# A two-layer hybrid trunk on one core: another order of work in the kernel's first microseconds

## The reference, cut to what matters

```python
h = rmsnorm(x, norm1_g[l])
x = x + mixing_block(h, cos, sin, w_in[l], ...)      # p = h @ w_in, four branches on column groups of p,
                                                     # y_b = branch_b @ w_branch[b], gated by sigmoid(h @ w_gate), then @ w_o
h = rmsnorm(x, norm2_g[l])
x = x + hier_moe(h, ...)                             # 16 experts, top 1 group of 4, top 2 experts inside it
```

## Time and profile before

| what | value |
|---|---|
| timed runs, median (lowest to highest) | 839.33 us (838.76 to 840.03), 3 runs |
| the profiled execution's own time | 837.2 us |
| its span, first to last instruction | 835.5 us |
| PE busy | 789.1 us, 94% |
| DVE busy / ACT busy / POOL busy | 79% / 61% / 2% |
| mean granted clock of TensorE | 0.975 of full speed |
| read from memory | 188.12 MB |

### The profile page before, as it was taken

The page is one execution under the profiler, slowest core; times in us unless marked ns, Lnnn a source line. Parts: engine busy times, 40 slices in busy tenths (PEclk is TensorE's granted clock), DMA queues, the critical chain, the costliest instruction groups (busy, mean ns, idle before and its releaser), DMA issues.

```text
span 835.5 us, 13286 instructions
## 1 busy us (share of the span) xinstructions
PE 789.1 (94%) x4822; PEld 698.7 (84%) x4822; DVE 660.5 (79%) x854; ACT 512.1 (61%) x567; POOL 20.0 (2%) x32
## 2 busy tenths in 40 slices
PE   6999999999779999999799999999958999999996
PEld 6899999998558877877789999999846878787875
DVE  5858996497567889989774899559756889988987
ACT  5535555653537778777543555664454787878774
POOL 3110000000000000000001000000000000000000
PEclk9999999999879999999999999999987999999998
DMA  7867254366215999999645644337521899999994
GB/s 245 293 202 249 84 175 150 102 243 211 101 51 204 339 347 331 356 342 325 215 144 200 206 147 153 127 102 276 167 88 48 282 322 362 334 350 348 352 342 172
DMA packets 80309, 189.80 MB, mean 227 GB/s; under 512 B 12022, under 2 KB 23944, under 8 KB 80264
## 3 DMA queue, kind: packets, MB, share of 16 engines
q1 hardware_dynamic: 80264, 189.20, 65.5%
HBM read 188.12 MB, written 1.05 MB: 226 GB/s over the span
## 4 chain that ended last, share of the span: by engine, by line
PE 63%; issue 23%; ACT 5%; DVE 5%; DMA 2%; POOL 1%; SPq 0%; ACTq 0%; DVEq 0%; POOLq 0%
PE bank L1244 18%; PE bank L1246 18%; PE bank L1245 18%; ACT w_hi L482 3%; PE bank L1539 2%; PE bank L1568 2%; DVE w_lo L743 2%; PE bank L1593 1%; DMA raw<-in_w_in 1%; DMA raw<-in_w_e_up 1%; DMA raw<-in_w_e_down 1%; PE bank L1512 1%; ACT xn L493 1%; ACT a_hi L661 0%; DVE gates L1180 0%
## 5 line engine op out<-in xcount | busy, mean ns | idle before, releaser
L743 DVE TENSOR_TENSOR w_lo<-raw,w_hi 128x2048 fp32r<-128x2048 f32 (+1 forms) x183 | 403.1, 2217 | 91.8 <-ACT w_hi L482 90.7
L482 ACT ACTIVATE w_hi<-raw 128x2048 fp32r<-128x2048 f32 (+1 forms) x183 | 338.8, 1857 | 180.5 <-PE bank L1246 136.6
L1244 PE MATMUL bank<-a_hi,w_hi 128*128 128x256 f32 x704 | 201.2, 286 | 4.0 <-DVE a_lo L818 4.0
L1245 PE MATMUL bank<-a_hi,w_lo 128*128 128x256 f32 x704 | 199.8, 284 | 0.0
L1246 PE MATMUL bank<-a_lo,w_hi 128*128 128x256 f32 x704 | 199.7, 284 | 0.0
L1244 PE MATMUL bank<-w_hi,y_lo 128*128 128x512 f32 x432 | 171.4, 397 | 0.5 <-DVE w_lo L743 0.2
L1246 PE MATMUL bank<-w_lo,y_lo 128*128 128x512 f32 x432 | 168.8, 391 | 0.0
L1244 PEld LDWEIGHTS bank<-a_hi,w_hi 128*128 128x128 f32 x704 | 135.6, 193 | 5.2 <-DVE w_lo L743 3.6
L1245 PEld LDWEIGHTS bank<-a_hi,w_lo 128*128 128x128 f32 x704 | 135.7, 193 | 0.1
L1246 PEld LDWEIGHTS bank<-a_lo,w_hi 128*128 128x128 f32 x704 | 135.6, 193 | 0.0
L1245 PE MATMUL bank<-w_hi,y_hi 128*128 128x512 f32 x288 | 112.3, 390 | 0.0
(11 more groups left out here) (288 smaller groups left out, 872.2 us busy)
## 6 DMA issues: line engine op xcount, KB each, us to landing
raw<-in_w_e_gate SPq DMA_DIRECT2D x72, 512.0 KB, 4.4
raw<-in_w_e_up SPq DMA_DIRECT2D x72, 512.0 KB, 5.8
raw<-in_w_e_down SPq DMA_DIRECT2D x72, 512.0 KB, 4.9
raw<-in_w_gate SPq DMA_DIRECT2D x56, 512.0 KB, 4.6
raw<-in_w_in SPq DMA_DIRECT2D x38, 512.0 KB, 6.5
raw<-in_w_branch SPq DMA_DIRECT2D x16, 512.0 KB, 4.1
raw<-in_w_o SPq DMA_DIRECT2D x16, 512.0 KB, 4.2
raw<-in_w_gate SPq DMA_DIRECT2D x16, 256.0 KB, 2.9
```

What stands on the lines that cost most here:

```text
L482: a.activation(w_hi[:, at.slot(n, PART), 0:w], raw[:, slot, 0:w], ACT.Copy).then_inc(hi_done, 1)
L743: v.tensor_tensor(w_lo[:, part, 0:w], raw[:, slot, 0:w], w_hi[:, part, 0:w].bitcast(F32), ALU.subtract).then_inc(split_done, 1)
L1244: mm(ps, a2[0], b2[0], start=first, stop=False, skip_group_check=shared)
L1245: mm(ps, a2[1], b2[0], start=False, stop=False, skip_group_check=shared)
```

## The change

- SP: unit 0 is requested right behind x; then come g1, units 1 and 2, unit 3 (which stood behind all parameters), `positions` (which stood ahead of g1), and then the parameters.
- ACT: an activation of one element right at the start, whose function is the one that x's squares use, so that the function table is loaded there. Unit 3's `hi` stands ahead of the sine of the angles.
- DVE: `lo` of unit 0 stands behind the fourth slice of h_lo, no longer ahead of the first. `lo` of unit 3 stands ahead of the rotary angles.
- PE: in layer 0 six more products of ones (`keep_warm(3, 6)`) follow the transposes, into bank 3. Units 0 and 1 are multiplied in another order: first all products with w_hi (hi*hi and h_lo*w_hi; 32 matmuls), which wait for `hi` alone, then those with w_lo (16 matmuls), which wait for `lo`. The products and their number are as before.

```diff
             for t in range(T):
                 sp.dma_start(x[:, t, :], x_in[0, P * t:P * t + P, :]).then_inc(x_loaded[t], 16)
-            sp.dma_start(posi[:, :], positions[0].rearrange("(t p) -> p t", p=P),
-                         allow_slow_non_contiguous=True).then_inc(pos_loaded, 16)
...
+            load(At(0, 0, False), 0, *units_a[0], 0)
             norm_gains(0)
-            first_units(At(0, 0, False), 0)
+            first_units(At(0, 0, False), 0, 1)
+            load(At(0, 0, False), AHEAD, *units_a[AHEAD], 0)
+            sp.dma_start(posi[:, :], positions[0].rearrange("(t p) -> p t", p=P),
+                         allow_slow_non_contiguous=True).then_inc(pos_loaded, 16)
             mixer_parameters(0)
             router_parameters(0)
...
+            act.wait_ge(pool_consts, 1)
+            a.activation(warm[:, 0:1], ones[0:1, 0:1], ACT.Square)
             act.wait_ge(S("ssq_zero"), 1)
...
                     hi(at, 1)
                     hi(at, 2)
+                    hi(at, AHEAD)
                     act.wait_ge(S("angles"), 1)
...
-            lo(At(0, 0, False), 0)
...
+                    if l == 0 and k == 3:
+                        lo(At(0, 0, False), 0)
...
                     lo(at, 1)
                     lo(at, 2)
+                    lo(at, 3)
                     rope_angles()
...
+                if l == 0:
+                    keep_warm(3, 6)
...
+                def first_products(at, n, h, wp):
+                    ks = [4 * h + kk for kk in range(4)]
+                    pe.wait_ge(hi_done, at.unit(n) + 1)
+                    for kk, k in enumerate(ks):
+                        pe.wait_ge(S("h_lo_done"), KT * l + k + 1)
+                        for hp in H:
+                            for f in range(2):
+                                mm(bank[0][:, 256 * f:256 * f + 256], wp[0][:, kk, P * f:P * f + P], hp[:, k, :],
+                                   start=k == 0 and f == 0 and hp is h_hi, stop=False, skip_group_check=True)
+                            for t in range(T):
+                                mm(bank[1][:, 256 * t:256 * t + 256], hp[:, k, P * t:P * t + P], wp[0][:, kk, 256:512],
+                                   start=k == 0 and t == 0 and hp is h_hi, stop=False, skip_group_check=True)
+                    ready(at, n)
+                    for kk, k in enumerate(ks):
+                        ...
+                    return last
...
+                        if l == 0 and b == 0:
+                            first_products(at, n, h, wp).then_inc(unit_used, 1)
+                            continue
```

More of the change, by code:

```diff
@@ L358, in load, with first_units @@
                     sp.dma_start(d, s).then_inc(landed[slot], 16)
-            def first_units(at, l):
-                for n in range(AHEAD):
+            def first_units(at, l, n0=0):
+                for n in range(n0, AHEAD):
                     load(at, n, *units_a[n], l)
+            load(At(0, 0, False), 0, *units_a[0], 0)
             norm_gains(0)
-            first_units(At(0, 0, False), 0)
+            first_units(At(0, 0, False), 0, 1)
+            load(At(0, 0, False), AHEAD, *units_a[AHEAD], 0)
+            sp.dma_start(posi[:, :], positions[0].rearrange("(t p) -> p t", p=P),
+                         allow_slow_non_contiguous=True).then_inc(pos_loaded, 16)
             mixer_parameters(0)
@@ L371, in _ @@
                 at = At(l, before, False)
-                for n in range(AHEAD, NA):
+                for n in range(AHEAD if l else AHEAD + 1, NA):
                     load(at, n, *units_a[n], l)
@@ L520, in _ @@
                     hi(at, 2)
+                    hi(at, AHEAD)
                     act.wait_ge(S("angles"), 1)
                     a.activation(cos_sin[:, :, :, :], rope[:, 0, 0:2, 0:2, :], ACT.Sin).then_inc(S("rope_ready"), 1)
-                for n in range(AHEAD, 6):
+                for n in range(AHEAD if l else AHEAD + 1, 6):
                     hi(at, n)
@@ L830, in _ @@
                 step.at(n_first + DVE_STEPS * l)
-                lo(at, 3)
+                if l:
+                    lo(at, 3)
                 lo(at, 4)
@@ L1296, in channels @@
                                  both(H, k), first and fb == 0, last, True)
+                def first_products(at, n, h, wp):
[12 more added lines that the diff above has]
+                    for kk, k in enumerate(ks):
+                        for f in range(2):
+                            mm(bank[0][:, 256 * f:256 * f + 256], wp[1][:, kk, P * f:P * f + P], h_hi[:, k, :],
+                               start=False, stop=k == KT - 1, skip_group_check=True)
+                        for t in range(T):
+                            last = mm(bank[1][:, 256 * t:256 * t + 256], h_hi[:, k, P * t:P * t + P], wp[1][:, kk, 256:512],
+                                      start=False, stop=k == KT - 1, skip_group_check=True)
+                    return last
                 for b in range(4):
@@ L1304, in _ @@
                             parameter_columns()
+                        wp = parts(at, n, "p (c m) -> p c m", c=4)
+                        if l == 0 and b == 0:
+                            first_products(at, n, h, wp).then_inc(unit_used, 1)
+                            continue
                         ready(at, n)
-                        wp = parts(at, n, "p (c m) -> p c m", c=4)
                         for kk in range(4):
```

## The result

The changed kernel took 833.26 us (median of 4 runs, 831.70 to 835.83) against 839.68 us for the kernel before in the same comparison (4 runs, 838.76 to 841.26): ratio 0.9925, 95% interval 0.9902 to 0.9947. The forecast of 836.1 us had the direction right and the size wrong: 3.2 us were forecast, 6.4 lie between the medians, and the stated range reached down only to 835.0. The interval of the ratio stands for a gain of 4.5 to 8.2 us. Two further comparisons of the same kernel, with 11 and 12 runs, gave 0.9939 (0.9913 to 0.9965) and 0.9936 (0.9914 to 0.9958), which is 5.1 and 5.4 us; the medians themselves lie 4.6 and 5.6 us apart (834.97 against 839.52, 834.41 against 839.99). All three intervals hold 5 us, so nothing shows that the first comparison's 6.4 was more than its draw of four runs.

What follows compares the result with a forecast made beforehand. PE was taken to bound the kernel from its first product on. First product 1.8 us earlier plus cold start gone, 1.4, made 3.2: 839.33 to 836.1 us (own range 835.5 to 836.7; 8 in 10: 835.0 to 837.6).

Steps and rivals of the forecast that it cites:

- What bounds the kernel: Whole kernel: PE, busy 94% of the span, never waits from its first product at 15.27 up to 100 us.
- The order of the products: Units 0 and 1: with `lo` (2.29 us) no longer in front, the first product could start 2.97 us after `hi` starts.
- Six products of ones: PE behind x's transposes: 12 matmuls about 0.214 us apart take 2.57 us and hold PE to 13.5.
- the unit's earlier request: SP's load of unit 0: second half requested 0.98 us earlier, landing between 9.5 and 10.47; no visible effect, only cover.
- rival 4: Start of PE: x scaled sooner or ones quicker, first product at 12.5; gain 4.2 us, time 835.1; chance 7%.
- I carry the difference over: From profile to median: timed median lies 2.1 us above the profiled execution, so 839.33 - 3.2 = 836.1.
- x's landing: Load queues at the start: unit 0's megabyte right behind x costs 0 to about 1 us, taken as 0.15; transposes at 10.0.
- rival 3: Load of x: lands 1 us later than taken, first product at 14.5; gain 2.2 us, time 837.1; chance 13%.
- The cold start: The 96 matmuls of units 0 and 1: 11.5 us at the upper clock level instead of 12.92, gaining 1.4 us.
- The other covers: Later work: parameters land by 21.2, needed at 25.0; sine at 28.3; Gelu at 33.4; none delays PE.
- forecast margin of 2.2: Banks for unit 4: Gelu done by about 34.8, PE wants the banks at 37.0, 2.2 us to spare.

## Why the prediction was right in kind and wrong in size

**What bounds the kernel** was right: PE from its first product on, and what is gained ahead of it is still there at unit 4 (4.66) and at 92 us (4.63).

**The order of the products** was right within 0.03 us, but the forecast didn't let it decide. It worked out 2.97 us from `hi`'s start to the first product. It is 2.94 in seven profiles (9.03 to 11.97, 8.97 to 11.91, 9.89 to 12.83, 10.07 to 13.01, 10.16 to 13.10, 9.93 to 12.87, 10.40 to 13.34); the old order has 4.78 or 4.79 in four (10.49 to 15.27, 11.47 to 16.25, 10.22 to 15.00, 8.90 to 13.69). `lo` off the chain is worth 1.84 us.

**The step that failed** is "*Six products of ones*": 2.57 us, "and hold PE to 13.5". They take 1.3 us, from the first one's issue to that of the first product (10.67 to 11.97), and the run with twelve of them shows the price by itself. The 0.214 us came from the 28 matmuls at the start. Their spacing is twice the 0.108 of the later ones, the same factor as between the two levels of the clock (0.50 and 1.00 in the windows), so they most likely ran at the lower level; no granted clock below 1.00 is recorded there, and I had taken the 1.00 in the window from 5 to 6 as a reading. Two rows of the trace after show that the column can't be read so there: PE's matmuls go from 6 in that window, as the earlier trace rows has it, to 9 and 10 per us, and the column stays at 1.00.

```profile
5.00:6.00 1.00, 1.00 (x9) 1.00 (x9) 0.21 (x1) 0.91 (x3) 0.09 (x1) 1.00 0.87 303
6.00:7.00 1.00, 1.00 (x10) 0.82 (x8) 0.21 (x2) 0.75 (x2) 0.47 (x1) 1.00 0.96 313
```

The check was at hand in the same rows: eight float32 matmuls of the same shape, the transposes of x, take 1.09 us, and the forecast itself put their issue at 0.93, 0.12 each. As it was, the term moved the binding branch. The forecast said that of the unit's earlier request "nothing is visible then". In fact the two branches ended together in the trace after and its first repetition (ones from 10.67 for 1.3, and h_lo from 11.34 for 0.62, both to 11.97), and where unit 0 landed later, as in the third profile of the changed kernel, PE waited 0.77 us for it. So unit 0's landing is on the chain, and the 1.46 us by which it moved in the first pair were needed for the gain: with `hi` at 10.49 the first product would have come at 13.4. With the right price the forecast's own steps give 10.0 + 0.93 + 1.3 = 12.2 for the branch of x and 12.5 for the unit's: a gain of 2.8 + 1.4 = 4.2 us. That is rival 4, quicker ones included, in mechanism and time, and it had been given 7%.

**The rest of the miss.** Two landings were put late as well. Unit 0 was expected at 9.5 at the earliest, and `hi` began at 9.03, which takes the first product from 12.5 to 11.97; the request is 0.98 us earlier, and the other 0.48 lie within the spread of that landing. The second square of x began at 5.60, not at 5.88, and the transposes at 9.74, not at 10.0. So the trace has 4.65 us where the forecast has 3.2. The way from a trace to the median failed too: "I carry the difference over" takes the beginning of the one profiled execution for that of all, and the second trace of the kernel before has it 2.36 us longer.

**x's landing** was forecast 0.15 late with up to 1 us more as a rival. It landed 3.5 and 4.3 after its requests in the trace after, against 3.4 and 4.4. In all ten profiles with the megabyte right behind x the second half took 4.1 to 4.3, against 4.1 to 4.4 in the four with small requests between. The means of the two groups differ by less than 0.1 us, though from 5 to 6 us, while x's second half landed, the queues moved 303 GB/s after the change and 107 before. The 0.15 was an estimate; any delay is below that spread, and rival 3's microsecond is out.

**The cold start** was 1.35 in the trace that was read (12.92 against 11.57 after) and 2.7 in the next (14.30 against 11.58), and 1.4 was put down as if it were fixed. The granted clock read 0.50 from 15 to 18 us in the first of these traces of the kernel before and from 16 to 22 in the second. The bridge did what it was to do: a clock of 1.00 from 8 to 36 us and 11.57 to 11.64 us for the 96 matmuls in nine profiles that have one (in the tenth, with `hi` in halves, waits lie between them). Without it, in the changed kernel, the clock fell in one of two (to 0.50 from 13 to 16 us).

**The other covers held.** The parameters never stopped PE. The sine of the angles began at 27.27 instead of 28.3, the Gelu began at 33.85 instead of 33.4, because ACT waited for units 4 and 5 to land, 0.28 and 0.92 us, which was not forecast; the last row that empties its banks ends at 35.17 and PE came to unit 4 at 35.51, so 0.3 us of the forecast margin of 2.2 were left. Nothing of it reached PE.

**From 4.65 to 6.4 or 5.2.** The pair of profiles gives 4.65 at the beginning; the second trace of the kernel before, against the second after, gives 7.06. The medians of the three comparisons (6.4, 4.6, 5.6) lie about there. What differs at the beginning is when unit 0 lands (`hi` at 10.49 and 11.47 before the change) and how long the clock stays down (3 and 6 us at 0.50); later on come stretches at the lower clock, in some executions and not in others. None of this has to be called on to explain 6.4, since 4.65 lies within the interval of each comparison. Whether the mean gain is larger than 4.65, and by what share of these two, stays open.

## What to carry to other kernels

Price an operation on TensorE by its own spacing and compare it with the same form elsewhere in the trace before using it: a clock column that reads full at the very start of a trace need not be the clock that the matmuls had (here it read 1.00 beside 6 and beside 10 matmuls per us). Where two branches end within a microsecond, work both out to the end, since a small error in one term decides which terms count at all. And one profiled execution is one draw: look for the steps of the chain that vary (here a landing, 8.90 to 10.40, and a cold start, 1.35 and 2.7), because what a change gains on average can differ from what it gains in the trace that was read.

## What the runs showed that was not expected

- The clock fell in one execution and stayed up in the other of the same kernel, after the same 2.3 us without products (the two profiles without the six products). It also began to fall (to 0.50) between 93 and 101 us, while PE was busy all the time, behind the thin matmuls named above, in six of the fourteen profiles, one of them of the kernel before, and not in the other eight.
- Unit 0's landing varied by 1.5 us (`hi` from 8.90 to 10.40) between executions with the same requests ahead of it, while the halves of x varied by 0.4 and 0.3 over all profiles.
- A power of one column on GpSimd took 1.39 to 1.44 us when DVE scaled x at the same time and 0.56 alone; both rows are in each of the fourteen traces, and no run varied it, so that DVE is the reason is not shown.
